# The weight blocks of a mixer's last projection: one f32 load, rounded on ScalarE and subtracted on VectorE, in place of two DMAs

## The chip, the cores and the metric

The kernel runs on one core of a Trainium2 chip. The metric is the device time in microseconds of one execution. The core has TensorE (matmuls), VectorE, ScalarE and GpSimd, and SyncE, which here only issues DMAs. Each engine works through its own program in order; semaphores connect them. DMAs are issued here from SyncE's and GpSimd's queues and move data between HBM and the on-chip memory.

## What is computed

Two layers of a streaming encoder on 512 tokens plus 16 meta tokens, width 1024, everything in float32:

```python
for i in range(DEPTH):                                   # DEPTH = 2
    h_res = h_res + 0.5 * swiglu(rms_norm(h_res, ffn1_norm[i]), ffn1_w_in[i], ffn1_w_out[i])
    h = rms_norm(h_res, mix_norm[i])
    proj = h @ w_in[i]
    y_a = conv_module(proj[..., :o_conv], ...)           # ends in  u @ conv_w_out
    ...
    y_b = window_sink_attention(q, k, v, attn_sinks[i]) @ attn_w_out[i]
    gates = jax.nn.sigmoid(proj[..., o_v:] + gate_bias[i])
    merged = gates[..., :D_MODEL] * y_a + gates[..., D_MODEL:] * y_b
    h_res = h_res + merged @ w_out[i]                    # the last projection of the mixer
    h_res = h_res + 0.5 * swiglu(rms_norm(h_res, ffn2_norm[i]), ffn2_w_in[i], ffn2_w_out[i])
return h_res[:, N_META:]
```

The change concerns the weights of `merged @ w_out[i]` alone.

## The kernel before

**Number format.** Every product is made of three TensorE passes on operands split in two: a rounded part (fp32r, "hi") and the rest ("lo"). A product is hi x hi + hi x lo + lo x hi. Activations and weights alike need both parts in on-chip memory.

**Mixer.** The weights of a layer's mixer come in 68 blocks of 128 output columns by 1024 (512 KB each), numbered n: 44 of the input projection, then 8 each of `attn_w_out` (from `B_ATT`), `conv_w_out` (from `B_CONV`) and `w_out` (from `B_MO`). A block is used in 48 matmuls of 264 columns in layer 0 and in 24 of 512 columns in layer 1, where the meta tokens are dropped (line 1169, function `products`). The blocks go through four slots in turn (`MIX_UNITS`): block n may be fetched when TensorE has finished block n - 4 (`mix_freed`). `blk_used` counts TensorE's finished pieces.

**Two ways to a hi and a lo part.** Most blocks take the first:

- GpSimd's queue loads the block into the hi buffer `wha`, rounded on the way (`mix_hi`, line 648). ScalarE writes -hi into `wla` (`neg`, line 707). GpSimd's queue then loads the block a second time and adds it onto `wla` (`mix_lo`, line 652), which leaves the rest. TensorE waits for that DMA (`w_lo`).
- The eight blocks of `conv_w_out`, named by `WHOLE`, take the other: SyncE's queue loads the block once as f32 into `wfa` (`load_whole`, line 580), which is the same memory as `wla`. ScalarE rounds it into `wha` (`neg`, line 704). VectorE subtracts in place, `wla = wfa - wha` (`whole_lo`, line 2007), and TensorE waits for that (`cw_lo`).

**The order is written out by hand.** On GpSimd the plain load of block n stands ahead of the accumulating load of n - 1, and behind block `B_MO + 5` the first accumulating load of the next feed-forward stage (`base_lo`, line 638). On SyncE the loads of the eight `conv_w_out` blocks stand between the first loads of the next feed-forward's weight pairs (`load_pair`, lines 566 and 569, 768 and 256 KB). On ScalarE the instruction for block `B_MO + 3 + m` stands ahead of the work on block m's result.

**The last projection** on VectorE is `mixer_out`: for each block m, add TensorE's result onto the residual (line 1814, the eviction), then make the operands of the next feed-forward stage from it (`x7_operands`, with the sum of squares, lines 1530 and 1545 to 1559; ScalarE does its share in lines 787 to 804). For an odd m there is more to make than for an even one. After block 0 come four sums of weight tiles (`sum12`, `sum43`), after blocks 2 and 4 one subtraction for them (`sum_lo`, line 1593). The eight blocks m = 0 to 7 of this projection are called W0 to W7 in the prediction.

**Feed-forward.** Its 22 weight pairs a stage come through `raw` on SyncE, and are combined by VectorE, ScalarE and accumulating loads of GpSimd in the same manner.

Of the kernel before, what the change touches and what calls it, by code (L numbers as in the profile page):

```python
# [36 lines left out]
KD, KF = D // P, FF // P  # L37
# [47 lines left out]
B_CONV, B_MO = B_ATT + KD, B_ATT + 2 * KD  # L85
NBLK = B_MO + KD
T_MIX, T_ATT, T_CONV, T_MO = B_MIX, B_ATT, B_CONV, B_MO

MIX_UNITS = (6, 4, 0, 2)
WHOLE = range(B_CONV, B_CONV + KD)  # L90
SLOT_TURNS = (NBLK - len(WHOLE)) // 4
OUT_UNITS = ((2, 4, 0), (10, 12, 8))

# [69 lines left out]
def run_of(j):  # L163

    s = j // KF
    while not begins(s):
        s -= 1
    e = s + 1
    while e < STAGES and not begins(e):
        e += 1  # L170
    return s * KF, e * KF
# [72 lines left out]
def mix_freed(l, n):  # L244
    if n > 3:
        return USED["mix", l, n - 4]
    if n == 0:
        return USED["P4", (2 * l + 1) * KF - 1]
    if REGION[(2 * l + 1) * KF - 1] == 0:
        return USED[("P7", "P2", "P6")[n - 1], (2 * l + 1) * KF - 1]  # L250
    return USED["out", 2 * l, len(CHUNKS) - 1, NB - 4 + n]
# [16 lines left out]
def build(nc, x, params, qk_gain, sinks, pairs, outs6, outs5, mixes, out):  # L268
# [7 lines left out]
    with ctx:  # L276
# [3 lines left out]
        def sem(name):  # L280
            return ctx.enter_context(nc.semaphore(name))
# [116 lines left out]
        def units(bufs, u, n):  # L398

            t, u = (bufs[0], u) if u < BASE_UNITS else (bufs[1], u - BASE_UNITS)  # L400
            return t[:, u:u + n, :, :].rearrange("p u k c -> p (u k) c")
# [33 lines left out]
        def ps(n):  # L435

            return (n + 1) % 2
# [11 lines left out]
        def mix_units(bufs, n):  # L449
            return units(bufs, MIX_UNITS[n % 4], 2)  # L450

        def mix_turn(l, n):
            if n in WHOLE:
                return n % 4, (l * len(WHOLE) + n - B_CONV) // 4 + 1
            return n % 4, l * SLOT_TURNS + (n - (len(WHOLE) if n > B_CONV else 0)) // 4 + 1

        def split_count(l, n):

            return l * (NBLK - len(WHOLE)) + n + 1 - (len(WHOLE) if n > B_CONV else 0)

# [14 lines left out]
        cw_in, cw_hi, cw_lo = [sem(f"cw_in{s}") for s in range(4)], sem("cw_hi"), sem("cw_lo")  # L475
# [77 lines left out]
        def _(sp):  # L553
# [23 lines left out]
            def load_whole(l, n):  # L577
                s, _ = mix_turn(l, n)
                sp.wait_ge(blk_used, mix_freed(l, n))
                sp.dma_start(mix_units(f32_units, n), mixes[l * NBLK + n, :, :, :]).then_inc(cw_in[s], 16)  # L580
# [21 lines left out]
            for l in range(DEPTH):  # L602
# [4 lines left out]

                for n in WHOLE[0:5]:
                    load_whole(l, n)
# [14 lines left out]
        @block.gpsimd  # L624
        def _(pool):
            nc.gpsimd.memset(eps64[:, :], HD * EPS).then_inc(const_done, 1)
            nc.gpsimd.memset(ident[:, :], 0.0).then_inc(const_done, 1)
            nc.gpsimd.memset(ones[:, :], 1.0).then_inc(const_done, 1)
            nc.gpsimd.memset(eps1[:, :], EPS).then_inc(const_done, 1)
            pool.wait_ge(const_done, 4)  # L630
            nc.gpsimd.affine_select(out=ident[:, :], in_=ident[:, :], compare_op=ALU.not_equal, fill=1.0,
                                    base=0, pattern=[[-1, P]], channel_multiplier=1).then_inc(const_done, 1)

            def base_lo(j):
                pool.wait_ge(a_neg, j)
                pool.dma_start(units(lo_units, U_A[REGION[j]], 2), pairs[j, :, KP:3 * KP, :], accum_op=ALU.add)\
                    .then_inc(a_lo[j % 2], 16)

            def base22_lo(j):
                pool.wait_ge(a22_neg, j + 1)
                pool.dma_start(units(lo_units, U_A22[REGION[j]], 1), pairs[j, :, 0:KP, :], accum_op=ALU.add)\
                    .then_inc(a22_lo[j % 2], 16)

            def mix_hi(l, n):
                pool.wait_ge(blk_used, mix_freed(l, n))
                pool.dma_start(mix_units(hi_units, n), mixes[l * NBLK + n, :, :, :]).then_inc(w_hi[n % 4], 16)

            def mix_lo(l, n):  # L650
                pool.wait_ge(w_neg, split_count(l, n))
                pool.dma_start(mix_units(lo_units, n), mixes[l * NBLK + n, :, :, :], accum_op=ALU.add)\
                    .then_inc(w_lo[n % 4], 16)

            def stage(s):
                for c, (ta, tb) in enumerate(CHUNKS):
                    j0, j1 = s * KF + ta, s * KF + tb
                    more = j1 < run_of(j0)[1]
                    for j in range(j0, j1):
                        if j + 2 < j1:  # L660
                            base_lo(j + 2)
                        if j + 1 < j1:
                            base22_lo(j + 1)
                    if more:
                        base_lo(j1)
                        base22_lo(j1)
                        base_lo(j1 + 1)

            base22_lo(0)
            base_lo(1)  # L670
            for l in range(DEPTH):
                stage(2 * l)
                mix_hi(l, 0)
                mix_lo(l, 0)
                mix_hi(l, 1)
                for n in range(2, NBLK):
                    if n not in WHOLE:
                        mix_hi(l, n)
                    if n - 1 not in WHOLE:
                        mix_lo(l, n - 1)  # L680
                    if n == B_MO + 5:
                        base_lo((2 * l + 1) * KF)
                mix_lo(l, NBLK - 1)
                base22_lo((2 * l + 1) * KF)
                base_lo((2 * l + 1) * KF + 1)
                stage(2 * l + 1)
# [816 lines left out]
        def _(dve):  # L1503
# [28 lines left out]
            def x7_operands(l, which, s, m):  # L1532

                n = norm(l, which)
                a, w = of_pair(s * KF)
                kp, odd = divmod(m, 2)
                scr7 = x7_scratch(s, kp)
                part = lambda i, o=1: scr7[:, i * w:(i + o) * w]
                t3, t2, t4, b21, b22, t1, b11, b12 = (part(i) for i in range(8))
                k = s * KP + kp  # L1540

                def low(n, i, at, o):

                    dve.wait_ge(x7_hi, X7_PARTS * k + n)
                    tt(x7l[:, kp, i * w:(i + o) * w], part(at, o), x7h[:, kp, i * w:(i + o) * w].bitcast(F32),
                       ALU.subtract).then_inc(x7_lo, o // 2)

                dve.wait_ge(b_done, s * KD + m + 1)
                if not odd:
                    tt(t1, b11, b12, ALU.subtract).then_inc(t_step, 1)  # L1550
                    if s:
                        add_squares(n, m, a)
                        low(1, T1, 5, 2)
                    return
                tt(t3, b22, b12, ALU.subtract).then_inc(t_step, 1)
                dve.wait_ge(t_step, 4 * k + 1)
                stt(t2, t1, -1.0, b22, ALU.mult, ALU.subtract).then_inc(t_step, 1)
                dve.wait_ge(t_step, 4 * k + 3)
                stt(t4, t2, -1.0, b21, ALU.mult, ALU.subtract).then_inc(t_step, 1)
                low(2, B21, 3, 2 if s else 4)  # L1560
                if s:
                    add_squares(n, m, a)
                low(3, T3, 0, 3)
# [241 lines left out]
                        elif last and lw < DEPTH:  # L1805
                            x7_operands(lw, 0, s + 1, m)

            def mixer_out(l):
                j0 = (2 * l + 1) * KF
                post = l == LAST  # L1810
                nc.vector.memset(acc_m, 0.0).then_inc(acc_done, 2)
                for m in range(KD):
                    ready(l, B_MO + m)
                    stt(cols(resid[:, m, :], post), slot(ps(m), post), 0.5, cols(resid[:, m, :], post), ALU.mult,
                        ALU.add).then_inc(out_taken, 1)
                    x7_operands(l, 2, 2 * l + 1, m)
                    if m == 0:
                        sum12(j0)
                        sum43(j0)
                    if m in (2, 4):  # L1820
                        sum_lo(j0, m // 2 - 1)
# [127 lines left out]
            for l in range(DEPTH):  # L1949
# [50 lines left out]
                a = first(post)  # L2000

                def whole_lo(m):
                    if m >= KD:
                        return
                    n = B_CONV + m
                    dve.wait_ge(cw_hi, l * KD + m + 1)
                    tt(mix_units(lo_units, n), mix_units(f32_units, n), mix_units(hi_units, n).bitcast(F32),
                       ALU.subtract).then_inc(cw_lo, 1)

# [57 lines left out]
                for m in range(KD):  # L2067
# [7 lines left out]
                    dve.wait_ge(mg_hi, l * KD + m + 1)  # L2075
                    tt(ml[:, m, a:], t1[:, a:], mh[:, m, a:].bitcast(F32), ALU.subtract).then_inc(mg_lo, 1)
                    whole_lo(m + 2)
                mixer_out(l)
                ffn(l, 1)


# [51 lines left out]
```

## Time and profile before

| | us |
|---|---|
| median of 3 runs | 2333.5 |
| lowest, highest | 2332.78, 2334.3 |
| the profiled execution's own time | 2333.69 |
| its span, from the first to the last instruction | 2331.9 |
| TensorE busy | 2308.5 (99%) |
| VectorE busy | 1676.5 (72%) |
| ScalarE busy | 1245.2 (53%) |
| GpSimd's queue: MB moved, share of the 16 DMA engines | 194.54, 41.5% |
| SyncE's queue: MB moved, share of the 16 DMA engines | 153.47, 22.4% |

The granted clock of TensorE has a mean of 0.999 of its full 2.4 GHz. The last projection runs from about 788.6 to 835.3 us in layer 0 and from about 1938 to 1984.9 us in layer 1. In the views, PE is TensorE, PEld its loading of weights, DVE is VectorE, ACT ScalarE, POOL GpSimd and SP SyncE; L1169 is line 1169 of the kernel. An instruction's record gives its start and duration; in brackets stands how long its engine was idle just before it and what ended that. Consecutive records on VectorE can overlap by a little. A wait matters for the time only where TensorE, or what TensorE waits for, does the waiting.

### The profile page before, as it was taken

The numbers are of one execution on the slowest core, as the hardware profiler recorded it, in microseconds if no ns is written. First come the engines' busy times: TensorE is split into PE (matmuls) and PEld (weight loads), VectorE is DVE, ScalarE is ACT, GpSimd is POOL, SyncE is SP. The second block draws the span as 40 slices with busy tenths as digits, with TensorE's granted clock in tenths as the row PEclk, the third lists the DMA queues.
The fourth block names the chain that finished last, engine by engine and source line by source line (L and its number), as shares of the span: only waits on it lengthen the run. The fifth ranks groups of instructions, "written<-read, shape, count | busy, mean of one in ns | idle before, by whom it ended". The sixth has DMA issues, their size and how long they took to land.

```text
span 2331.9 us, 43089 instructions
## 1 busy us (share of the span) xinstructions
PE 2308.5 (99%) x17685; PEld 2202.1 (94%) x17685; DVE 1676.5 (72%) x2761; ACT 1245.2 (53%) x2029; POOL 324.5 (14%) x424
## 2 busy tenths in 40 slices
PE   7999999999999999999999999999999999999999
PEld 6999999999999999999999999999888787998997
DVE  7855754798896588567788557548998865874863
ACT  8734733554455477357567347334545455762751
POOL 1100101211211111011011011011212202110110
PEclk9999999999999999999999999999999999999999
DMA  6855836777676768468458457367777657773853
GB/s 188 183 129 137 177 90 147 151 166 151 149 147 164 170 143 185 112 147 185 116 132 182 129 134 178 90 150 156 160 167 154 152 162 175 166 179 103 180 126 110
DMA packets 109347, 351.09 MB, mean 151 GB/s; under 512 B 12384, under 2 KB 12384, under 8 KB 109152
## 3 DMA queue, kind: packets, MB, share of 16 engines
q0 software_dynamic: 59760, 194.54, 41.5%
q1 hardware_dynamic: 49024, 153.47, 22.4%
q8 instruction: 140, 2.29, 0.4%
q14 instruction: 55, 0.45, 0.1%
q10 hardware_dynamic: 368, 0.33, 0.0%
HBM read 343.80 MB, written 2.10 MB: 148 GB/s over the span
## 4 chain that ended last, share of the span: by engine, by line
PE 93%; DVE 2%; DMA 1%; issue 1%; ACT 1%; DVEq 0%; POOL 0%; ACTq 0%
PE po L1169 33%; PE po L1186 23%; PE po L1237 22%; PE ptr L1186 7%; PE pov L1186 5%; PE pstat L1385 1%; PE pov L1424 1%; PE pov L1427 1%; DMA wla<-in_mixes 1%; DMA wha<-in_mixes 1%; PE ptr L1394 1%; DVE rms L1666 0%; DVE wla L1593 0%; PE pstat L1350 0%; ACT whb L716 0%
## 5 line engine op out<-in xcount | busy, mean ns | idle before, releaser
L1169 PE MATMUL po<-xh,wha 128*128 128x264 f32 (+1 forms) x1408 | 344.3, 311 | 0.0
L1169 PE MATMUL po<-xl,wha 128*128 128x264 f32 (+1 forms) x1408 | 335.5, 305 | 0.0
L1169 PE MATMUL po<-xh,wla 128*128 128x264 f32 (+1 forms) x1408 | 334.8, 304 | 0.0
L1834 DVE SCALAR_TENSOR_TENSOR cv<-ub,lp,cv 128x528 f32<-128x528 f32 (+1 forms) x480 | 333.1, 751 | 1.7
L1237 PE MATMUL po<-hh,wla 128*128 128x264 f32 (+1 forms) x1232 | 283.7, 300 | 0.0
L1237 PE MATMUL po<-hl,wha 128*128 128x264 f32 (+1 forms) x1232 | 283.7, 300 | 0.0
L1237 PE MATMUL po<-hh,wha 128*128 128x264 f32 (+1 forms) x1232 | 282.4, 299 | 0.0
L1601 DVE TENSOR_TENSOR wla<-wfa,wha 128x768 fp32r<-128x768 f32 (+1 forms) x128 | 113.2, 889 | 197.0 <-ACT wha L745 196.9
L1169 PEld LDWEIGHTS po<-xh,wha 128*128 128x128 f32 x1408 | 227.0, 188 | 17.6 <-issue 1.8
L745 ACT ACTIVATE wha<-wfa 128x768 fp32r<-128x768 f32 (+1 forms) x128 | 101.0, 789 | 262.1 <-DMA wfa<-in_outs 262.1
L1169 PEld LDWEIGHTS po<-xh,wla 128*128 128x128 f32 x1408 | 226.4, 188 | 11.0
L1186 PE MATMUL po<-x7h,wha 128*128 128x264 f32 (+1 forms) x832 | 236.2, 284 | 0.4 <-DVE wla L1593 0.4
L1169 PEld LDWEIGHTS po<-xl,wha 128*128 128x128 f32 x1408 | 226.7, 188 | 10.1
L1186 PE MATMUL po<-x7h,wla 128*128 128x264 f32 (+1 forms) x832 | 236.0, 284 | 0.0
L1186 PE MATMUL po<-x7l,wha 128*128 128x264 f32 (+1 forms) x832 | 236.0, 284 | 0.0
L707 ACT ACTIVATE wla<-wha 128x1024 fp32r<-128x1024 f32 x120 | 127.1, 1059 | 188.8 <-DMA wha<-in_mixes 188.7
L1186 PE MATMUL po<-x7h,whb 128*128 128x264 f32 (+1 forms) x768 | 219.8, 286 | 3.0 <-ACT tmp L758 3.0
L1186 PE MATMUL po<-x7l,whb 128*128 128x264 f32 (+1 forms) x768 | 218.2, 284 | 0.0
L1186 PE MATMUL po<-x7h,wlb 128*128 128x264 f32 (+1 forms) x768 | 217.8, 284 | 0.0
L1237 PEld LDWEIGHTS po<-hh,wla 128*128 128x128 f32 x1232 | 196.9, 189 | 7.5
L1237 PEld LDWEIGHTS po<-hl,wha 128*128 128x128 f32 x1232 | 196.4, 188 | 7.5
L1237 PEld LDWEIGHTS po<-hh,wha 128*128 128x128 f32 x1232 | 196.1, 188 | 7.9
(258 smaller groups left out, 5651.8 us busy)
## 6 DMA issues: line engine op xcount, KB each, us to landing
raw<-in_pairs SPq DMA_DIRECT2D x88, 768.0 KB, 5.3
wha<-in_mixes POOLq DMA_DIRECT2D x120, 512.0 KB, 4.3
wla<-in_mixes POOLq DMA_DIRECT2D x120, 512.0 KB, 6.6
wfa<-in_outs SPq DMA_DIRECT2D x64, 384.0 KB, 3.1
wlb<-in_pairs POOLq DMA_DIRECT2D x47, 512.0 KB, 8.3
raw<-in_pairs SPq DMA_DIRECT2D x88, 256.0 KB, 6.6
wla<-in_pairs POOLq DMA_DIRECT2D x88, 256.0 KB, 6.4
wla<-in_pairs POOLq DMA_DIRECT2D x40, 512.0 KB, 8.4
```

The lines of the kernel that those rows point to most:

```text
L707: func(mix_units(lo_units, n), mix_units(hi_units, n).bitcast(F32), ACT.Copy, scale=-1.0)\
L745: func(units(hi_units, u, 2)[:, 0:k, :], units(f32_units, u, 2)[:, 0:k, :], ACT.Copy).then_inc(ob_hi, 1)
L1169: ins = mm(po[:, 2 * out_slot + h, 0:width], w[:, k, :], v[:, k, t:t + width], start=begin and k == 0 and p == 0, stop=last and k == kt - ...
L1186: ins = mm(bank, a[:, kp, :], b[:, kp, cols7], start=begin and kp == 0 and p == 0, stop=kp == KP - 1 and p == 2, skip_group_check=True)
L1237: ins = mm(po[:, 2 * ps(m) + h, 0:width], w[:, k, :], v[:, t, x:x + width], start=t == 0 and p == 0, stop=t == CHUNK_T - 1 and p == 2, ski ...
L1385: ins = mm(score(i, h), q[r, :], kw[r, c:c + WK], start=True, stop=True)
L1394: ins = tr(ptr[:, (2 * n + h) * P:(2 * n + h + 1) * P], pw[:, (b + 1) % 2, at:at + WIN], ident[:, :])
L1424: mm(dst[h * HD:(h + 1) * HD], vw[:, pos - 1, :], cut(pt[:, i, h, :]), start=True, stop=False, skip_group_check=True)
L1427: ins = mm(dst[h * HD:(h + 1) * HD], vz[:, i, h, :], cut(ptm[:, :]), start=pos == 0, stop=True, skip_group_check=True)
L1601: tt(units(lo_units, u, 2)[:, 0:k, :], units(f32_units, u, 2)[:, 0:k, :], units(hi_units, u, 2)[:, 0:k, :].bitcast(F32), ALU.subtract).the ...
L1834: stt(cv[:, j, a:], u, w, cv[:, j, a:], ALU.mult, ALU.add).then_inc(conv_step, 1)
```

## The change

`WHOLE` is extended to the end of the list, so the eight `w_out` blocks of each layer take the second way too. Sixteen blocks in all lose two DMAs on GpSimd's queue each and get one on SyncE's; ScalarE writes hi instead of -hi, an instruction of the same size; VectorE gets one subtraction for each.

```diff
-WHOLE = range(B_CONV, B_CONV + KD)
+WHOLE = range(B_CONV, NBLK)
...
                     if n == B_MO + 5:
                         base_lo((2 * l + 1) * KF)
-                mix_lo(l, NBLK - 1)
                 base22_lo((2 * l + 1) * KF)
...
-            def mixer_out(l):
+            def mixer_out(l, whole_lo):
...
                     x7_operands(l, 2, 2 * l + 1, m)
+                    if KD + m + 2 < len(WHOLE):
+                        whole_lo(KD + m + 2)
                     if m == 0:
                         sum12(j0)
...
                 def whole_lo(m):
-                    if m >= KD:
-                        return
                     n = B_CONV + m
-                    dve.wait_ge(cw_hi, l * KD + m + 1)
+                    dve.wait_ge(cw_hi, l * len(WHOLE) + m + 1)
...
-                mixer_out(l)
+                mixer_out(l, whole_lo)
```

`SLOT_TURNS` and the counts in `mix_turn` and `split_count` follow from `len(WHOLE)`. After the second edit the changed kernel's line numbers differ by one or two from those of before.

VectorE, layer 0, in the last projection, from the eviction of block 0 to that of block 2. Before:

```order
L1814 SCALAR_TENSOR_TENSOR resid<-po,resid 128x528
L1550 TENSOR_TENSOR tmp<-tmp 128x264
L1530 TENSOR_TENSOR pw<-pw 128x528
L1545 TENSOR_TENSOR x7l<-tmp,x7h 128x528
L1573 TENSOR_TENSOR wfb<-raw 128x512
...
L1586 TENSOR_TENSOR wfb<-raw 128x512
L1814 SCALAR_TENSOR_TENSOR resid<-po,resid 128x528
L1555 TENSOR_TENSOR tmp<-tmp 128x264
...
L1545 TENSOR_TENSOR x7l<-tmp,x7h 128x792
L1814 SCALAR_TENSOR_TENSOR resid<-po,resid 128x528
```

The same place now:

```order
L1813 SCALAR_TENSOR_TENSOR resid<-po,resid 128x528
L1549 TENSOR_TENSOR tmp<-tmp 128x264
L1529 TENSOR_TENSOR pw<-pw 128x528
L1544 TENSOR_TENSOR x7l<-tmp,x7h 128x528
L2006 TENSOR_TENSOR wla<-wfa,wha 128x1024
L1572 TENSOR_TENSOR wfb<-raw 128x512
...
L1585 TENSOR_TENSOR wfb<-raw 128x512
L1813 SCALAR_TENSOR_TENSOR resid<-po,resid 128x528
L1554 TENSOR_TENSOR tmp<-tmp 128x264
...
L1544 TENSOR_TENSOR x7l<-tmp,x7h 128x792
L2006 TENSOR_TENSOR wla<-wfa,wha 128x1024
L1813 SCALAR_TENSOR_TENSOR resid<-po,resid 128x528
```

The subtraction for block m + 2 now stands between the last operand made from block m and the eviction of block m + 1, with m = 0 ahead of the four sums.

GpSimd, layer 0, from the accumulating load of block 4 to the loads of the next stage. Before:

```order
L652 DMA wla<-in_mixes 128x1024
L638 DMA wlb<-in_pairs 128x1024
L648 DMA wha<-in_mixes 128x1024
L652 DMA wla<-in_mixes 128x1024
L648 DMA wha<-in_mixes 128x1024
L652 DMA wla<-in_mixes 128x1024 x2
L643 DMA wla<-in_pairs 128x512
L638 DMA wla<-in_pairs 128x1024
```

Now, behind the last block of `attn_w_out`:

```order
L652 DMA wla<-in_mixes 128x1024 x2
L638 DMA wlb<-in_pairs 128x1024
L643 DMA wla<-in_pairs 128x512
L638 DMA wla<-in_pairs 128x1024
```

All loads of the `w_out` blocks are gone from between the loads for the next stage.

SyncE, layer 0, from the fifth load of a `conv_w_out` block on. Before:

```order
L566 DMA raw<-in_pairs 128x1536
L569 DMA raw<-in_pairs 128x512
L580 DMA wfa<-in_mixes 128x1024 x2
L566 DMA raw<-in_pairs 128x1536
L569 DMA raw<-in_pairs 128x512
```

Now:

```order
L566 DMA raw<-in_pairs 128x1536
L569 DMA raw<-in_pairs 128x512
L580 DMA wfa<-in_mixes 128x1024 x10
L566 DMA raw<-in_pairs 128x1536
L569 DMA raw<-in_pairs 128x512
```

The third pair of the next stage is now fetched behind the load of block 7, which waits until TensorE has finished block 3.

## Rows read from the trace of the kernel before

**Rows 1.** The page's first part: engine, busy us (share of span), instructions.

```profile
PE 2308.5 (99%) x17685; PEld 2202.1 (94%) x17685; DVE 1676.5 (72%) x2761; ACT 1245.2 (53%) x2029; POOL 324.5 (14%) x424
```

**Rows 2.** TensorE's waits over the whole span: total us, times, longest.

```profile
PE po L1169 <- DMA wla<-in_mixes: 2.0, 4, 0.7
```

**Rows 3.** Timeline, TensorE, layer 0: first matmuls of W2 and W3.

```profile
800.26 0.42 PE L1169 MATMUL po<-mh,wha 128*128 128x264 f32 x2
...
806.10 0.42 PE L1169 MATMUL po<-mh,wha 128*128 128x264 f32 x2
```

**Rows 4.** Timeline, TensorE, layer 1: first matmuls of W2 to W6.

```profile
1949.10 0.40 PE L1169 MATMUL po<-mh,wha 128*128 128x512 f32 x1
...
1954.67 0.40 PE L1169 MATMUL po<-mh,wha 128*128 128x512 f32 x1
...
1961.09 0.47 PE L1169 MATMUL po<-mh,wha 128*128 128x512 f32 x1 [0.68 <-DMA wla<-in_mixes]
...
1967.62 0.47 PE L1169 MATMUL po<-mh,wha 128*128 128x512 f32 x1 [0.71 <-DMA wla<-in_mixes]
...
1973.63 0.47 PE L1169 MATMUL po<-mh,wha 128*128 128x512 f32 x1 [0.20 <-DMA wla<-in_mixes]
```

**Rows 5.** Timeline, VectorE, layer 0: W0's and W1's evictions, each with its last operand.

```profile
794.62 0.71 DVE L1814 SCALAR_TENSOR_TENSOR resid<-po,resid 128x528 f32<-128x528 f32 x1 [2.39 <-PE po L1169]
...
797.29 0.70 DVE L1545 TENSOR_TENSOR x7l<-tmp,x7h 128x528 fp32r<-128x528 f32 x1
...
800.57 0.70 DVE L1814 SCALAR_TENSOR_TENSOR resid<-po,resid 128x528 f32<-128x528 f32 x1
...
804.47 0.97 DVE L1545 TENSOR_TENSOR x7l<-tmp,x7h 128x792 fp32r<-128x792 f32 x1
```

**Rows 6.** Timeline, VectorE, layer 1: W1's eviction and its last operand.

```profile
1949.60 0.68 DVE L1814 SCALAR_TENSOR_TENSOR resid<-po,resid 128x512 f32<-128x512 f32 x1
...
1953.42 0.95 DVE L1545 TENSOR_TENSOR x7l<-tmp,x7h 128x768 fp32r<-128x768 f32 x1
```

**Rows 7.** Timeline: a subtraction of 1024, what follows it, TensorE behind one.

```profile
36.42 1.16 DVE L1593 TENSOR_TENSOR wla<-wfa,wha 128x1024 fp32r<-128x1024 f32 x1
...
37.64 0.39 PE L1186 MATMUL po<-x7h,wha 128*128 128x264 f32 x1 [0.45 <-DVE wla L1593]
...
37.87 0.29 PE L1186 MATMUL po<-x7l,wha 128*128 128x264 f32 x1
...
812.38 1.22 DVE L1593 TENSOR_TENSOR wlb<-wfb,whb 128x1024 fp32r<-128x1024 f32 x1
813.51 0.70 DVE L1814 SCALAR_TENSOR_TENSOR resid<-po,resid 128x528 f32<-128x528 f32 x1
```

**Rows 8.** Timeline, ScalarE: its instruction for W5 in layers 0 and 1.

```profile
808.88 1.06 ACT L707 ACTIVATE wla<-wha 128x1024 fp32r<-128x1024 f32 x1 [3.71 <-DMA wha<-in_mixes]
...
1958.69 1.06 ACT L707 ACTIVATE wla<-wha 128x1024 fp32r<-128x1024 f32 x1 [4.56 <-DMA wha<-in_mixes]
```

**Rows 9.** DMA issues (KB each, median us to landing), then issues in the timeline.

```profile
wlb<-in_pairs POOLq DMA_DIRECT2D x47, 512.0 KB, 8.3
...
wfa<-in_mixes SPq DMA_DIRECT2D x16, 512.0 KB, 3.6
...
800.73 0.54 POOL L648 DMA_DIRECT2D wha<-in_mixes  x1 [4.25 <-PE po L1169]
...
1949.56 0.54 POOL L648 DMA_DIRECT2D wha<-in_mixes  x1 [3.99 <-PE po L1169]
1950.09 0.91 POOL L652 DMA_DIRECT2D wla<-in_mixes  x1
1950.64 1.25 POOL L638 DMA_DIRECT2D wlb<-in_pairs  x1
...
1949.76 0.33 SPq L566 DMA_DIRECT2D raw<-in_pairs  x1
```

**Rows 10.** Timeline, VectorE, layer 0: first sum for the stage's second pair.

```profile
840.87 0.68 DVE L1573 TENSOR_TENSOR wfa<-raw 128x512 f32<-128x512 f32 x1
```

## The prediction

> **What bounds the kernel now.** I read the page first: TensorE is busy for 2308.5 us, 99% of the span, so only what makes TensorE wait, or stops making it wait, can move the time [rows 1]. The view to read next is therefore the waits of TensorE. All of the mixer's products together waited 2.0 us for the second DMA of a weight block, in four waits [rows 2]. The change touches the eight blocks of the last projection in each of the two layers, called W0 to W7 here. In layer 0 they run without a gap: W2 begins at 800.26, W3 at 806.10, which gives 5.84 us a block [rows 3]. In layer 1 a block takes 1954.67 - 1949.10 = 5.57 us, and three blocks start late: W4 at 1961.09 instead of 1954.67 + 5.57 = 1960.24 (0.85 late), W5 at 1967.62 instead of 1966.66 (0.96), W6 at 1973.63 instead of 1973.19 (0.44) [rows 4]. Refilling after the last of these adds 0.07 (its first matmul is 0.47 long instead of 0.40); after the others it is in the next difference. The whole loss is 0.85 + 0.96 + 0.44 + 0.07 = **2.32 us**, all in layer 1. That is the most that the removed DMAs can give back.
>
> **What is removed.** Sixteen blocks no longer wait for GpSimd's queue, on which the plain copy of a later block, the accumulating copy of an earlier one and the first accumulating load of the next feed-forward stage stand in one line. In layer 1 the second copy of W4 and W5's first, next to 768 KB for the feed-forward pair on SyncE and 512 KB for it on GpSimd, were issued within about 1.1 us [rows 9]; ScalarE got W5's first copy only at 1958.69, 9.1 us after its issue at 1949.56 [rows 8, 9]. After the change W5's load is issued at about the same time (its slot is the same), while W4's second copy does not exist and the 768 KB come after W7's load in SyncE's program, some 11 us later; their first reader stands behind the sums of the pair before, which in layer 0 begin at 840.87 [rows 10], so this delay is free. A 512 KB load on SyncE landed in a median of 3.6 us [rows 9]. From slot free to block ready the copies need 3.6 + 1.1 (ScalarE) + 1.2 (VectorE) us if nobody is busy, against three blocks of 5.57 us until the block is used. The loads are covered. I take back the full 2.32 us. ScalarE's instruction is of the same size as before, on the same place: nothing.
>
> **What is added: VectorE, 16 x 1.22 us, and where it stands.** An existing subtraction of the same shape takes 1.22 us [rows 7]; in a row of work it costs 812.38 to 813.51 = 1.13 us, since the next instruction starts 0.09 before its record ends [rows 7]. The sum of 16 is 18 us, but VectorE is not the bound, so what counts is who waits. Two of each layer's eight (W0, W1) fall in the loop before, where VectorE waits for TensorE: nothing. For W2 to W7 the order is fixed: block Wm is taken over, its operands for the next stage are made, and only then comes the subtraction for W(m+2). TensorE wants that block one block after it finished Wm. So the price is the length of that chain against 5.84 or 5.57 us. A late W(m+2) is a new wait.
>
> *Even m.* From the eviction at 794.62 to the last operand's start at 797.29 are 2.67 us, and that instruction takes 0.70 [rows 5]. With the subtraction 2.67 + 0.70 - 0.09 + 1.22 = 4.50 us: it fits under 5.57. Nothing, also with the 1.13 us of the sum's low part that follows at m = 2 and 4.
>
> *Odd m.* In layer 0 the eviction at 800.57 is followed by the last operand at 804.47, 0.97 long: 3.90 + 0.97 - 0.09 = 4.78; with the subtraction 6.00 us [rows 5]. In layer 1, from 1949.60 to 1953.42 with 0.95 at the end: 3.82 + 0.95 - 0.09 = 4.68, with the subtraction 5.90 us [rows 6]. TensorE's matmul came 0.06 us after the end of such a subtraction (36.42 + 1.16 = 37.58, then 37.64) and lost 0.1 more in refilling (the next came 0.23 later, while 48 matmuls in 5.84 us make a pitch of 0.12) [rows 3, 7]. The eviction starts 0.20 after TensorE's block boundary (794.62 against 800.26 - 5.84 = 794.42) [rows 3, 5].
>
> - W5 and W7 in layer 0: 0.20 + 6.00 + 0.06 - 5.84 = 0.42, with refilling 0.52 each. In layer 1: 0.20 + 5.90 + 0.06 - 5.57 = 0.59, with refilling 0.69 each.
> - W3 is worse. W2's subtraction and then four sums for the next stage (four instructions from VectorE's order, about 0.69 each) stand ahead of W1's eviction, which already starts only when VectorE is free, at 800.57. It moves by 1.13 to 801.70. W3 is then ready at 801.70 + 6.00 + 0.06 = 807.76 against 806.10: 1.66, with refilling 1.76. In layer 1: 1949.60 + 1.13 + 5.90 + 0.06 = 1956.69 against 1954.67: 2.02, with refilling 2.12.
>
> Sum added: layer 0 1.76 + 2 x 0.52 = 2.80; layer 1 2.12 + 2 x 0.69 = 3.50; together 6.30 us. None of it hides behind a wait that was there, since the old waits (W4, W5, W6 of layer 1) had another cause. I checked what is late next: after W3 VectorE begins W2's eviction at once (1956.54), ends W4's subtraction at 1956.54 + 4.50 = 1961.04 and the low sum 1.13 later, at 1962.2, before TensorE finishes W3 (1956.69 + 0.10 + 5.57 = 1962.36). So the delay does not grow, but the cover is only 0.2 us there. Everything behind W7 hangs on TensorE and shifts as a whole.
>
> The cost of one uncovered subtraction has bounds. From below it is nothing, if VectorE were free when W(m+2) is wanted, as for even m; from above it is the whole 1.22 per odd block plus one more 1.13 for W2's in the way, that is 6 x 1.32 + 2 x 1.13 = 10.2 us. The gaps worked out above lie between, because 4.98 of 5.84 us were already used by the odd chain. I use these, since each is a difference of starts in one row of work.
>
> **Sum.** Against the profiled execution's own time: 2333.69 - 2.32 + 6.30 = 2337.67. It lies 0.19 above the median of the runs, 2333.5, so I name 2337.5 us, 0.17% more. A difference of this kernel under about 0.2%, 4.7 us, can hardly be told from no change; the forecast is just inside that.
>
> **Rivals.**
> - *W5's load lands late (slower).* GpSimd's 512 KB for the feed-forward are issued about 1 us before W5's load and share the engines with it: the 512 KB loads of that kind took a median of 8.3 us [rows 9]. ScalarE must round W5 before it starts on W2's takeover, at 1956.54 + 0.72 = 1957.3, so the load must land by 1956.2, 7.0 us after its slot is free at 1949.15. If it needs 9.1 us as the plain copy did [rows 8, 9], ScalarE is 2.0 us late; 0.85 reaches W4 and, as VectorE is then 0.6 behind, 0.6 reaches W5; in layer 0, with 8.2 us (800.73 to 808.88 [rows 8, 9]), 0.45 reaches W5. That is 1.9 more: 2339.5. For it: the same moment was the crowded one. Against it: two of the transfers that made the crowd, 1.25 MB, are no longer there. The rule decides from 7.0 us on. The Trainium skill (DMA: Bandwidth & Descriptors, SWDGE vs HWDGE vs iDMA) says that the two kinds of queue feed different inner queues of a DMA engine, which takes them in turn; by that, W5's load would be slowed to about half speed while the other runs, some 3.6 + 3.6 = 7.2 us with this trace's median, right at the limit, for perhaps 0.2 us.
> - *Only W3 waits.* If the odd chain is a little tighter than its records (the 0.20 and 0.09 are small differences), W5 and W7 wait for almost nothing: 1.76 + 2.12 - 2.32 = +1.56, 2335.2. Against it: the gap of 0.4 to 0.6 us is larger than the spread of any of these starts.
> - *VectorE is never missed.* Then the old waits go and nothing comes: 2331.4. It would need W1's eviction not to wait for the sums, which the 800.57 contradicts [rows 5].
> - *The delay grows.* If the 0.2 us of cover at W4 in layer 1 are used up, each later block inherits the rest: the next odd blocks wait up to 1.13 longer, twice or three times: about 2340.5.
>
> **How the numbers follow.** Forecast 0.62; late load 0.12; only W3 0.13; never missed 0.03; the delay grows 0.10. The range of 8 in 10 leaves out the never-missed case and the top of the growing one: 2335.0 to 2339.8. The line for slower by 0.2% is at 2338.2. A fifth of the forecast's own share lies above it (0.13), with nearly all of the late load and the growing delay (0.20): 0.33. Faster by over 0.2% is below 2328.8, which needs more than all waits found: 0.02. Same: 0.65.
>
> **What would show it.** In the changed profile TensorE's waits for the second DMA in the last projection are gone, and instead it waits for VectorE's subtraction in W3, W5 and W7 of both layers: about 1.7, 0.4, 0.4 us in layer 0 and 2.0, 0.6, 0.6 in layer 1, six waits and no others there. The odd chain reads 6.0 and 5.9 us from eviction to the end of the subtraction. ScalarE's wait before rounding W5 is short, and the 768 KB load is issued behind W7's. It is wrong if W4 or W6 wait, if W3's gap is not 1.7 to 2.1 us, or if the time moves anywhere else than in these two stretches.

## The result and the profile after

The changed kernel takes 2337.93 us in the median of 7 runs (2336.76 to 2341.61), the kernel before 2333.26 beside it (7 runs, 2331.01 to 2334.30). The medians lie 4.7 us (0.20%) apart. The ratio of the two series, worked out from all their executions, is 1.0026, with a 95% interval of 1.0016 to 1.0035: slower. It is larger than the ratio of the medians since three of the seven executions took 2340.17 us or more. The forecast was 2337.5. The profiled execution took 2337.86 us, its span is 2336.1. A second series of the same changed kernel gave 2337.97 us against 2333.07, ratio 1.0022 (1.0013 to 1.0032).

The first part of the page answers to [rows 1]: TensorE is as busy as before, VectorE works 19 us more, GpSimd 23 us less.

```profile
PE 2308.3 (99%) x17685; PEld 2201.5 (94%) x17685; DVE 1695.6 (73%) x2777; ACT 1245.0 (53%) x2029; POOL 301.2 (13%) x392
```

The waits of TensorE, over the whole span (total us, times, longest), answer to [rows 2]. In the place of three of the four waits for `wla<-in_mixes` there are six for VectorE's subtraction, 5.3 us; the one that is left comes at 711 us, before the last projection. The 1.5 us for `wlb` in the other row stand at the kernel's start, outside the change. The profile before lacks them because TensorE ran there at half clock (granted 0.54 between 22 and 24 us) and was late itself; its next matmul that waits for VectorE comes at 37.64 us before and at 37.68 after.

```profile
PE po L1168 <- DVE wla L2006: 5.3, 6, 1.9
...
PE po L1185 <- DVE wlb L1592: 1.5, 1, 1.5
PE po L1168 <- DMA wla<-in_mixes: 0.5, 1, 0.5
```

The timeline of TensorE shows where they are: the first matmuls of W3, W5 and W7, in layer 0 and then in layer 1. These answer to [rows 3] and [rows 4]. No other block begins late.

```profile
807.62 0.48 PE L1168 MATMUL po<-mh,wha 128*128 128x264 f32 x2 [1.61 <-DVE wla L2006]
...
819.91 0.48 PE L1168 MATMUL po<-mh,wha 128*128 128x264 f32 x2 [0.38 <-DVE wla L2006]
...
832.20 0.49 PE L1168 MATMUL po<-mh,wha 128*128 128x264 f32 x2 [0.38 <-DVE wla L2006]
...
1959.51 0.47 PE L1168 MATMUL po<-mh,wha 128*128 128x512 f32 x1 [1.95 <-DVE wla L2006]
...
1971.41 0.47 PE L1168 MATMUL po<-mh,wha 128*128 128x512 f32 x1 [0.52 <-DVE wla L2006]
...
1983.32 0.47 PE L1168 MATMUL po<-mh,wha 128*128 128x512 f32 x1 [0.52 <-DVE wla L2006]
```

VectorE's timeline of layer 0 shows why, beside [rows 5]: the subtraction for W2 (797.66) and four sums (the last at 800.86) stand ahead of W1's eviction at 801.46, and W3's subtraction ends at 806.26 + 1.22 = 807.48, after W1's last operand. TensorE's matmul of W3 comes at 807.62.

```profile
797.66 1.22 DVE L2006 TENSOR_TENSOR wla<-wfa,wha 128x1024 fp32r<-128x1024 f32 x1
...
800.86 0.68 DVE L1585 TENSOR_TENSOR wfb<-raw 128x512 f32<-128x512 f32 x1
801.46 0.70 DVE L1813 SCALAR_TENSOR_TENSOR resid<-po,resid 128x528 f32<-128x528 f32 x1
802.96 0.43 DVE L1554 TENSOR_TENSOR tmp<-tmp 128x264 f32<-128x264 f32 x1 [0.81 <-ACT tmp L786]
...
805.37 0.98 DVE L1544 TENSOR_TENSOR x7l<-tmp,x7h 128x792 fp32r<-128x792 f32 x1
806.26 1.22 DVE L2006 TENSOR_TENSOR wla<-wfa,wha 128x1024 fp32r<-128x1024 f32 x1
```

TensorE's first matmuls at the edges of the two stretches show where the 4.2 us of span went (us, from its timeline):

| stretch | before | after | difference |
|---|---|---|---|
| span's start to W0, layer 0 | 788.61 | 788.35 | -0.26 |
| W0 to the end of W7, layer 0 | 46.69 | 49.76 | **+3.07** |
| from there to W0, layer 1 | 1102.65 | 1102.56 | -0.09 |
| W0 to the end of W7, layer 1 | 46.90 | 48.30 | **+1.40** |
| the rest | 347.05 | 347.13 | +0.08 |

### The profile page after: what moved, and what is told of

Same layout as the page of the kernel before. It is cut to its first block, busy times and chain, and to the rows that moved or that the text cites. A ratio compares the mean times of both kernels' runs of the same rounds, so it can differ in the third digit from the quotient of the medians.

```text
span 2336.1 us, 43089 instructions
## 1 busy us (share of the span) xinstructions
PE 2308.3 (99%) x17685; PEld 2201.5 (94%) x17685; DVE 1695.6 (73%) x2777; ACT 1245.0 (53%) x2029; POOL 301.2 (13%) x392
## 4 chain that ended last, share of the span: by engine, by line
PE 92%; DVE 4%; issue 1%; ACT 1%; DMA 0%; DVEq 0%; POOL 0%; ACTq 0%
PE po L1168 32%; PE po L1185 23%; PE po L1236 22%; PE ptr L1185 7%; PE pov L1185 5%; PE pstat L1384 1%; PE pov L1423 1%; DVE x7l L1544 1%; PE pov L1426 1%; PE ptr L1393 1%; DVE wla L2006 0%; DVE rms L1665 0%; ACT tmp L786 0%; DVE wla L1592 0%; DMA wla<-in_mixes 0%
## 5 line engine op out<-in xcount | busy, mean ns | idle before, releaser
L706 ACT ACTIVATE wla<-wha 128x1024 fp32r<-128x1024 f32 x104 | 110.2, 1060 | 154.4 <-DMA wha<-in_mixes 154.4
```

Source lines behind the costliest of these rows:

```text
L706: func(mix_units(lo_units, n), mix_units(hi_units, n).bitcast(F32), ACT.Copy, scale=-1.0)\
```

## The experiments

Two theories stood against each other. *Chain*: TensorE waits because the subtraction for W(m+2) comes at the end of a chain on VectorE that is longer than a block. *Load*: VectorE has more to do, or the blocks arrive later. Two more questions were what the waits before the change came from, and whether a late load of W5 could cost more. All times of a kernel are medians. Each ratio is to the kernel before, run beside it, and is worked out from all executions of both.

**e1_early: the subtraction right behind the eviction.**

```diff
+                    if KD + m + 2 < len(WHOLE):
+                        whole_lo(KD + m + 2)
                     x7_operands(l, 2, 2 * l + 1, m)
-                    if KD + m + 2 < len(WHOLE):
-                        whole_lo(KD + m + 2)
```

> The changed kernel with one call moved: VectorE subtracts for W(m+2) right behind the eviction of Wm, ahead of the operands, instead of behind them. Chain theory: TensorE waited only because the subtraction stood at the end of a chain of 6.0 us. Now the block is ready some 2.1 us after TensorE's boundary, VectorE fills the 0.8 us in which it waited for ScalarE anyway, and the odd chain grows from 4.8 to about 5.0 us, still under 5.57. No wait in W3, W5, W7, and the 2.3 us of DMA waits stay gone: 2331.0 us against 2333.3 before the change, 0.1% less. Rival, that the late blocks come from late loads or from VectorE having more to do: the waits stay, 2337 to 2338 us.

Measured: 2331.22 us (11 runs, 2330.59 to 2332.35) against 2332.46 before, ratio 0.9995 (0.9986 to 1.0004). Each of the two stretches has no wait of TensorE at all; W0 to the end of W7 takes 46.69 us in layer 0 and 44.58 in layer 1. In VectorE's timeline of layer 0 the subtraction (801.32) fills the time in which VectorE waited 0.81 us for ScalarE in the changed kernel (802.96 there):

```profile
800.70 0.70 DVE L1813 SCALAR_TENSOR_TENSOR resid<-po,resid 128x528 f32<-128x528 f32 x1
801.32 1.21 DVE L2006 TENSOR_TENSOR wla<-wfa,wha 128x1024 fp32r<-128x1024 f32 x1
802.45 0.42 DVE L1554 TENSOR_TENSOR tmp<-tmp 128x264 f32<-128x264 f32 x1
...
804.84 0.98 DVE L1544 TENSOR_TENSOR x7l<-tmp,x7h 128x792 fp32r<-128x792 f32 x1
```

The first operand starts 1.75 us after the eviction, against 1.50 in the changed kernel. So a subtraction of 1.22 us costs the chain 0.25, and W3 is ready at 802.53. The same instructions and the same loads, in another order, cost TensorE nothing: this is the chain theory, and "load" falls. Against the kernel before the gain (0.05%) is not clear of the interval. Between the medians of the changed kernel and this one lie 6.7 us, of which 0.8 lie between the two series of the kernel before.

**e2_idle_sub: the kernel before, with subtractions that nobody waits for.**

```diff
                     x7_operands(l, 2, 2 * l + 1, m)
+                    if m < 6:
+                        spare = hl[:, 8:10, 0:512]
+                        tt(spare, spare.bitcast(F32), spare.bitcast(F32), ALU.subtract)
```

> The kernel before, plus a subtraction of 1024 elements a partition at the six places of each layer where the change puts one; nothing waits for it. It only adds VectorE's time. Chain theory: VectorE has the room, TensorE waits for nothing new; 2333.3 us as before, W3, W5 and W7 of layer 0 without a wait. Rival, that 18 us more work on VectorE slows the stage by itself (evictions later, operands later): part or all of the 6.3 us, 2335 to 2340 us.

Measured: 2333.49 us against 2332.46, ratio 1.0003 (0.9995 to 1.0012). In layer 0 all blocks follow each other at 5.84 us; in layer 1 only a wait for a DMA is left (0.59 us, W5). So the work alone, twelve subtractions at the very places where they cost 6.8 us when TensorE waits for them, makes no block of the last projection late.

It is not quite free, though. Behind the projection of layer 1 TensorE waits for an operand made from W7, which it does in no other profile:

```profile
1988.48 0.38 PE L1186 MATMUL pov<-x7h,whb 128*128 128x256 f32 x1 [1.09 <-DVE x7l L1545]
```

From the end of W7 to the end of the span are 348.65 us here and 347.05 in the kernel before. The same profile gains 1.50 us in the stretch ahead of it (45.40 instead of 46.90), since the DMA waits happened to be shorter. The unchanged time is the sum of these two.

**e3_w2_ahead: W2's subtraction ahead of the first eviction.**

```diff
-                    if KD + m + 2 < len(WHOLE):
+                    if m and KD + m + 2 < len(WHOLE):
                         whole_lo(KD + m + 2)
...
+                whole_lo(KD + 2)
                 mixer_out(l, whole_lo)
```

> The changed kernel, with W2's subtraction moved ahead of the first eviction, so that it no longer stands before the four sums. Chain theory: W1's eviction comes 1.13 us sooner in both layers, so W3's waits fall from 1.61 to about 0.5 and from 1.95 to about 0.8 us; the others stay: 2337.9 - 2.26 = 2335.7 us. Rival, that W3 waits for its own load or rounding: 1.61 and 1.95 stay, 2337.9 us.

Measured: 2335.61 us against 2332.46, ratio 1.0015 (1.0006 to 1.0024). TensorE's timeline, first matmuls of W3 in both layers:

```profile
806.18 0.48 PE L1168 MATMUL po<-mh,wha 128*128 128x264 f32 x2 [0.48 <-DVE wla L2006]
...
1956.88 0.47 PE L1168 MATMUL po<-mh,wha 128*128 128x512 f32 x1 [0.81 <-DVE wla L2006]
```

The two waits fell by 1.13 and 1.14 us, the 1.13 us that the subtraction takes in a row of work and that no longer stand before W1's eviction. W7's stayed at 0.38 and 0.52, W5's went from 0.38 to 0.47 in layer 0 and stayed at 0.52 in layer 1. The term for W3 in the sum was rightly built.

**e4_m1_early: only W3's subtraction moved ahead of the operands.**

```diff
+                    if m == 1:
+                        whole_lo(KD + 3)
                     x7_operands(l, 2, 2 * l + 1, m)
-                    if KD + m + 2 < len(WHOLE):
+                    if m != 1 and KD + m + 2 < len(WHOLE):
                         whole_lo(KD + m + 2)
```

> The changed kernel with only W3's subtraction moved ahead of the operands of W1; the other five stay. Chain theory: W3's waits (1.61 and 1.95 idle, 1.8 and 2.2 with refilling) go, W5's and W7's stay at 0.38 and 0.52: 2337.9 - 4.0 = 2333.9 us, about as before the change. Rival, that the wait moves on to the next odd block: W5 waits longer by what W3 loses, 2337 us.

Measured: 2335.60 us against 2334.07, ratio 1.0006 (0.9997 to 1.0015). The two stretches, 48.75 and 46.84 us, are together 2.5 us shorter than in the changed kernel, not 4.0. W3's waits are gone, but W5's grew:

```profile
818.39 0.48 PE L1168 MATMUL po<-mh,wha 128*128 128x264 f32 x2 [1.00 <-DVE wla L2008]
830.68 0.48 PE L1168 MATMUL po<-mh,wha 128*128 128x264 f32 x2 [0.37 <-DVE wla L2008]
...
1969.27 0.47 PE L1168 MATMUL po<-mh,wha 128*128 128x512 f32 x1 [1.12 <-DVE wla L2008]
```

My expectation missed that W3's wait had given the engines behind it time. Without it W2's result comes 2 us sooner, while ScalarE is still kept by W5's load, and VectorE by ScalarE (ScalarE's and VectorE's timelines, layer 0):

```profile
806.46 1.06 ACT L703 ACTIVATE wha<-wfa 128x1024 fp32r<-128x1024 f32 x1 [0.70 <-DMA wfa<-in_mixes]
807.42 0.72 ACT L786 ACTIVATE tmp<-resid,lp 128x528 f32<-128x528 f32 x1
...
808.18 0.43 DVE L1549 TENSOR_TENSOR tmp<-tmp 128x264 f32<-128x264 f32 x1 [1.52 <-ACT tmp L786]
```

The wait of 1.52 us is 0.72 longer than the usual 0.80, and W5's wait grew by 0.62. The rival of the moving wait was right for a third of the sum.

**e5_pair_later: the kernel before, with the 768 KB load held back.**

```diff
                     for t in range(ta, tb):
                         j = s * KF + t
+                        if s % 2 and t == 0:
+                            sp.wait_ge(blk_used, USED["mix", s // 2, B_MO + 3])
                         if j + 2 < run_of(j)[1]:
                             load_pair(j + 2)
```

> The kernel before, with SyncE's 768 KB load for the third pair of the next stage held back until TensorE has finished W3, as the change does by its order. It tells what the waits of layer 1 before the change came from. If from the crowd of four transfers at 1949.6 to 1950.7 us: W4's wait (0.68) goes and with it most of W5's and W6's, about -2 us, 2331 us. If from the order of GpSimd's queue (copy of W5 ahead of the second copy of W4, each waited for): the waits stay within 0.3 us, 2333 us.

Measured: 2331.45 us (11 runs, 2330.86 to 2332.71) against 2334.07, ratio 0.9991 (0.9982 to 1.0000). No wait is left in the last projection of either layer; layer 1's stretch takes 44.59 us instead of 46.90. The DMA issues between 1935 and 1990 us (KB each, median us to landing), first of the kernel before, then of this one:

```profile
wha<-in_mixes POOLq DMA_DIRECT2D x5, 512.0 KB, 8.0
...
wlb<-in_pairs POOLq DMA_DIRECT2D x1, 512.0 KB, 12.8
```

```profile
wha<-in_mixes POOLq DMA_DIRECT2D x5, 512.0 KB, 5.6
...
wlb<-in_pairs POOLq DMA_DIRECT2D x1, 512.0 KB, 9.8
```

So the 2.3 us that the change takes away come from four transfers issued within 1.1 us, not from the queue's order as such. One wait on SyncE takes them away too, with no work on VectorE. What the crowd costs differs between executions: in e2's profile, with the same four transfers, W5's first copy landed after 5.1 us instead of 9.1, and the stretch lost 0.8 us instead of 2.3.

**e6_longer: half a subtraction more ahead of each.**

```diff
                     if KD + m + 2 < len(WHOLE):
+                        spare = hl[:, 8, 0:512]
+                        tt(spare, spare.bitcast(F32), spare.bitcast(F32), ALU.subtract)
                         whole_lo(KD + m + 2)
```

> The changed kernel with an idle subtraction of 512 elements (0.61 us in a row of work) ahead of each of the twelve subtractions in the last projection. Chain theory with its cover: W3 is 1.22 later in each layer (once ahead of the sums, once in its own chain), W5 and W7 0.61 later each; in layer 1 the even steps run out of their 0.5 us of room and add some 0.2 each. Together 2.4 + 2.9 = +5.3: 2343.2 us, no wait in W4 and W6. Rival, each added piece counts (the delay accumulates, no cover in even steps): 12 x 0.61 = 7.3 us, 2345.2 us, with waits in W4 and W6.

Measured: 2344.67 us (4 runs, 2342.17 to 2348.71), ratio 1.0055 (1.0039 to 1.0070), between both expectations. The waits separate them:

```profile
808.46 0.49 PE L1168 MATMUL po<-mh,wha 128*128 128x264 f32 x2 [2.82 <-DVE wla L2008]
...
822.89 0.48 PE L1168 MATMUL po<-mh,wha 128*128 128x264 f32 x2 [0.97 <-DVE wla L2008]
...
1965.07 0.47 PE L1168 MATMUL po<-mh,wha 128*128 128x512 f32 x1 [3.16 <-DVE wla L2008]
```

W3 waits 1.21 us longer in both layers (2 x 0.61), W5 0.59 and W7 0.60 longer, and W4 and W6 wait for nothing: the even steps still cover their part. That gives +4.8 us of waits. Another 1.5 of the 6.8 us by which this execution lies above the first profiled one of the changed kernel are something else, which the windows of the trace show (length, busy time and instructions of PE, PEld, DVE, ACT and POOL, then granted clock, DMA share, GB/s):

```profile
810.00:812.00 2.00, 2.00 (x11) 2.00 (x10) 1.90 (x4) 2.00 (x4) 0.00 (x0) 0.50 0.01 4
812.00:814.00 2.00, 2.00 (x14) 2.00 (x13) 2.00 (x3) 0.75 (x1) 0.00 (x0) 0.67 0.00 0
814.00:816.00 2.00, 2.00 (x19) 2.00 (x18) 0.48 (x1) 0.00 (x0) 0.00 (x0) 1.00 0.00 0
```

Right behind the wait of 2.8 us TensorE runs for about 3.4 us at half its clock (1.2 instead of 2.4 GHz). W3's block takes 7.45 us instead of 5.9.

**e7_pool_later: GpSimd's load held back.**

```diff
                     if n == B_MO + 5:
+                        pool.wait_ge(blk_used, USED["mix", l, B_MO + 2])
                         base_lo((2 * l + 1) * KF)
```

> The changed kernel, with GpSimd's first accumulating load of the next stage held back until TensorE has finished W2. W5's load then has the DMA engines for itself. It lands 3.6 us after its issue instead of 6.8 in layer 0, ScalarE's wait of 0.80 us before rounding W5 goes, and the time stays at 2337.9 us, since nothing that TensorE waits for hangs on it. Rival: W3's or W5's waits shrink with it and the time falls.

Measured: a single execution, 2338.99 us, so its time alone decides nothing. In the changed kernel W5's load landed 6.6 us after its issue (issued at 800.2) and ScalarE waited 0.80 us for it; here the load landed after 3.5 us, and ScalarE does not wait (first row: the changed kernel's ScalarE; second: this one's):

```profile
806.86 1.06 ACT L703 ACTIVATE wha<-wfa 128x1024 fp32r<-128x1024 f32 x1 [0.80 <-DMA wfa<-in_mixes]
```

```profile
805.48 1.04 ACT L704 ACTIVATE wha<-wfa 128x1024 fp32r<-128x1024 f32 x1
```

The six waits of TensorE are 1.61, 0.37, 0.38, 1.95, 0.50 and 0.50 us, as in the changed kernel. So GpSimd's transfer slowed the load, and in the changed kernel this did not matter. Layer 1's W3 ran at half clock here too, for 1.6 us more; without that the execution would be at 2337.4.

**e8_pair_first: W5's load behind the 768 KB.**

```diff
                 for n in WHOLE[6:]:
+                    if n == B_MO + 5:
+                        j = (2 * l + 1) * KF + 2
+                        sp.wait_ge(a_hi, j - 1)
+                        sp.wait_ge(s_sum, 4 * (j - 1))
+                        sp.dma_start(raw[:, j % 2, KP:4 * KP, :], pairs[j, :, KP:4 * KP, :]).then_inc(raw_in[j % 2], 16)
                     load_whole(l, n)
```

(and `load_pair` leaves this part of that pair out)

> The changed kernel, with the 768 KB of the third pair put back ahead of W5's load on SyncE's queue, so that this load lands late (about 9 to 10 us after its slot is free, and it is behind a wait for VectorE's sums). It tests the rival of the prediction: from about 7.0 us on ScalarE, which must round W5 before it works on W2's result, holds up VectorE. Expected: ScalarE 2.5 us late, W4 waits about 1 us and W5 about 1.5 longer in both layers, +4 to +5, 2342 us. If the landing of this load does not matter: 2337.9 us.

Measured: 2342.06 us (5 runs, 2340.57 to 2342.21) against 2334.07, ratio 1.0033 (1.0021 to 1.0045). ScalarE and TensorE, timelines:

```profile
809.02 1.06 ACT L709 ACTIVATE wha<-wfa 128x1024 fp32r<-128x1024 f32 x1 [2.79 <-DMA wfa<-in_mixes]
```

```profile
820.96 0.48 PE L1174 MATMUL po<-mh,wha 128*128 128x264 f32 x2 [1.01 <-DVE wla L2012]
...
1967.70 0.47 PE L1174 MATMUL po<-mh,wha 128*128 128x512 f32 x1 [0.33 <-DVE wla L2012]
1974.66 0.48 PE L1174 MATMUL po<-mh,wha 128*128 128x512 f32 x1 [1.13 <-DVE wla L2012]
```

W5's load is there about 9 us after its slot is free. The mechanism is as described: W4 waits in layer 1, W5 waits 0.6 longer in both. But the two stretches grew by 0.86 and 1.19 against the changed kernel, together 2.0 us, not by 4 to 5: I had ScalarE's delay reach TensorE twice. The expected total came about by chance; in the profiled execution 0.9 us more were waits for DMAs in the input projection (1.4 us in all, against 0.5).

**e10_changed_again and e9_only_w3: the half clock.** The first is the changed kernel itself. The second:

```diff
+                    if m != 1 and KD + m + 2 < len(WHOLE):
+                        whole_lo(KD + m + 2)
                     x7_operands(l, 2, 2 * l + 1, m)
-                    if KD + m + 2 < len(WHOLE):
-                        whole_lo(KD + m + 2)
+                    if m == 1:
+                        whole_lo(KD + 3)
```

> The changed kernel once more, with more executions. Two looks (the lengthened chain and the held-back GpSimd load) showed a stretch of some 3 us at half the granted clock right behind W3's wait, worth about 1.5 us; the first profile of the changed kernel had none, but three of its seven executions took 2340.2 to 2341.6. If such a stretch falls on some executions only, the times spread over 4 to 5 us: a lowest group near 2337.5 and others 1.6 or 3.2 higher, while the kernels without long waits spread over less than 2 us. Rival, that those three were disturbed by something else: all executions near 2337.9, within 2 us.

> The changed kernel with all subtractions of the last projection moved ahead of the operands but W3's, which stays behind them: only the two longest waits are left. W1's eviction still stands behind W2's subtraction and the four sums. Chain theory: W3 waits 1.6 and 1.9 us, nothing else waits, 2331.2 + 1.8 + 2.1 = 2335.1 us. If the half-clock stretch follows these waits, it is here too, in some executions: a spread of 3 us or more above 2335. If it needs the other waits, the spread is under 2 us, as in the kernel with only W5 and W7 late.

Measured, changed kernel again: 2336.90, 2337.18, 2337.34, 2337.39, 2337.97, 2338.92, 2339.80, 2340.26 and 2341.35 us. The profiled one is the 2338.92, and it has the half clock behind W3's wait of 1.94 us in layer 1, but not behind that of 1.61 in layer 0. TensorE's rows there (a matmul starts every 0.43 us instead of every 0.23), then one window:

```profile
1959.02 0.47 PE L1168 MATMUL po<-mh,wha 128*128 128x512 f32 x1 [1.94 <-DVE wla L2006]
1959.33 0.39 PE L1168 MATMUL po<-ml,wha 128*128 128x512 f32 x1
1959.56 0.53 PE L1168 MATMUL po<-mh,wla 128*128 128x512 f32 x1
1959.89 0.63 PE L1168 MATMUL po<-mh,wha 128*128 128x512 f32 x1
...
1962.45 0.63 PE L1168 MATMUL po<-mh,wha 128*128 128x512 f32 x1
1962.88 0.50 PE L1168 MATMUL po<-ml,wha 128*128 128x512 f32 x1
1963.21 0.39 PE L1168 MATMUL po<-mh,wla 128*128 128x512 f32 x1
```

```profile
1960.00:1962.00 2.00, 2.00 (x6) 1.54 (x5) 1.64 (x4) 2.00 (x4) 0.00 (x0) 0.50 0.07 27
```

W3 takes 7.21 us there, 5.64 in the first profile of the same kernel: 1.57 us. The kernel with only W3 late gave 2333.34 us (11 runs, 2332.84 to 2334.48), ratio 1.0001 (0.9992 to 1.0010), not 2335.1. I had forgotten that W2's subtraction, moved with the others, delays W1's eviction by 0.9 us less when it fills a gap; W3's waits were only 0.71 and 1.07 us. So these runs don't test the half clock at a wait of 1.6 to 1.9; they show a spread of 1.6 us at waits up to 1.1.

## Why the prediction was right, point by point

- *What bounds the kernel.* Right: all of the difference lies where TensorE waits in the last projection, +3.07 and +1.40, and 0.3 the other way elsewhere.
- *What is removed, 2.32 us.* Right in size for the profile that it was read from: the three late blocks of layer 1 [rows 4] are gone, in the changed kernel as in e1 and e5, where that stretch falls from 46.90 to 44.58 us. But one profile was taken for all executions: e2's lost only 0.8 us there. That the sum comes within 0.4 us of the median is therefore in part luck. The cause named for them, the crowd of transfers [rows 9], is shown by e5.
- *What is added, 6.30 us.* The places were all right, W3, W5 and W7 and no other. Measured it is 3.07 + (1.40 + 2.32) = 6.79. The missing 0.5 is in the main one term six times over: from the end of the subtraction to the matmul I took 0.06 us from the kernel's start [rows 7]; here it was 0.14 and 0.15 (807.48 to 807.62, 1959.36 to 1959.51). Refilling took 0.07 instead of 0.10, and the starts of the chain, a few hundredths later than worked out, made up for it. W3 comes 1.78 and 2.12 us later behind W0's first matmul than before, against the 1.66 and 2.02 worked out. The idle time in the records, 1.61 and 1.95, is less because the record of the matmul ahead reaches beyond the start of a next one in line; by it W3's gap in layer 0 lies just outside the 1.7 to 2.1 us that were named as a sign of being wrong.
- *W3's own term*, with the subtraction and the sums ahead of W1's eviction, was shown by e3: 1.13 us less in each layer.
- *The cover.* "Even steps cover" was right, in e6 even with 0.61 us more. That VectorE has room as such was shown by e1, and by e2 for every block of the projection; behind W7 of layer 1, which the prediction did not consider, the added work of e2 cost TensorE 1.6 us.
- *Rivals.* The late load did not come: it took 6.6 us in layer 0 and 5.5 in layer 1 where I put the limit at 7.0. e8 shows that its mechanism is real: with W5's load there some 9 us after its slot was free, in both layers, the price was 2.0 us, about as worked out in the prediction (1.9), while my later expectation of 4 to 5 was wrong. e4 shows it too: once W3 is early, ScalarE's wait for this load reaches W5. The rule of the Trainium skill (DMA: Bandwidth & Descriptors, SWDGE vs HWDGE vs iDMA), that a DMA engine takes the two kinds of queue in turn, fits the trace roughly: 6.6 and 5.5 us beside GpSimd's transfer, where my estimate by it was 7.2, and 3.5 and 3.4 us once e7 held that transfer back. That the engines take turns is not shown by it, only that the two transfers slow each other.
- *What it left out.* The half clock behind W3's wait is in no term. It is not in the first profile of the changed kernel nor in e8's, but it is in the second and in e6 and e7. Of the 16 executions of the changed kernel 9 lie between 2336.8 and 2338.0 us and 7 between 2338.9 and 2341.6, up to 4 us above. The one of these that has a profile owes 1.57 us to it. The mean granted clock that is on record for every execution points the same way: of the 7, four have 0.998, three 0.999 and none 1.000; of the 9, none has 0.998 and five have 1.000. The three executions of the kernel before that took 2335.75, 2336.16 and 2337.12 us have 0.998 too. But 2341.61 us came with 0.999, and 2332.98, an execution of the kernel before, with 0.998. So whether the others owe their time to it stays open: e1 to e5 and e9, whose waits are at most 1.1 us, spread over only 1.3 to 2.3 us in 10 or 11 runs each, but the kernel before, which has no long wait there either, spread over 4.3 to 5.6 us in its series of 19 to 27 runs. The prediction held it likelier (0.65) that the change would stay within 0.2%. The medians are just at that line and the ratio, 1.0026, is past it; of the 4.7 us between the medians the sum has 4.0 and the late matmul starts 0.5.

## What to carry to other kernels

When work is put on an engine with room, price the place and not the engine: find who waits for its result, and add up the chain from that one's last hand-over. Here 1.22 us behind the operands, twice in W3's chain, cost up to 2.1 us of TensorE's time, and the same 1.22 us ahead of them nothing, since they filled a wait for ScalarE. And before a transfer is traded for an instruction, look at what else is in flight when it is late: holding back one load that nobody needed yet gave about the same time (2331.45 us, ratio 0.9991) as the best arrangement of the new scheme (2331.22, ratio 0.9995).

## What the runs showed of the hardware

- In some executions TensorE's granted clock fell to half, from 2.4 to 1.2 GHz, 0.3 to 1.4 us after it had restarted from a wait (0.3 in e7, 0.7 in e10, 1.4 in e6), and stayed there for some 3.4 us. It was seen in the last projection behind waits of 2.82 (e6), 1.94 and 1.95 us (e10, e7), each time worth 1.5 to 1.6 us. It did not come behind 1.95 us in the first profile of the changed kernel, nor behind 1.94 in e8, nor behind 3.16 in e6, nor in this place behind any wait of up to 1.61 us. So a wait of 2 us can cost most of its own length again.
- The twelve profiles show such a stretch at the kernel's start as well, from about 22 us on. TensorE had just waited for ScalarE. The five that had waited 2.48 to 2.82 us have it (before, e4, e6, e8, e9), the seven that had waited 1.29 to 2.02 us do not. It cost nothing there: TensorE's matmul behind a later wait for VectorE came at 37.47 to 37.65 us with such a stretch and at 37.23 to 37.68 without.
- From the end of a VectorE instruction to the matmul that waited for it passed 0.05 to 0.06 us at the kernel's start and 0.14 to 0.15 in the six waits of the changed kernel, and the block behind such a wait took 0.07 us more.
- A 512 KB load on SyncE landed after 3.5 us with GpSimd's transfer held back (e7) and after 6.6 us beside an accumulating one of the same size on GpSimd (the changed kernel), both in layer 0.
